# Softmax weights turned by VectorE blocks and HBM instead of TensorE, in a four-layer encoder

## What is computed

```python
# memory attention, in every layer
logits = einsum('bshd,bmhd->bhsm', xq, km)          # 4 heads, 256 x 256
w = softmax(logits, -1)
mem_out = einsum('bhsm,bmhd->bshd', w, vm)
# differential attention, layers 0 and 3
logits = einsum('bqhmd,bkhmd->bmhqk', qb, k) + bias  # 6 heads, two maps each
probs = softmax(logits, -1)
w = probs[:, 0] - lam * probs[:, 1]
o = einsum('bhqk,bkhe->bqhe', w, v)
```

## Time and profile before

| | |
|---|---|
| Time, median of 3 runs | 1245.52 us (1245.37 to 1245.91) |
| Profiled execution: span from first to last instruction | 1244.7 us |
| The profiled execution's own time | not given apart from its span; the median is 0.8 us above the span |
| TensorE busy | 1235.2 us, 99% |
| VectorE busy | 1024.4 us, 82% |
| ACT busy | 730.3 us, 59% |
| DMA, 16 engines | 55.5% of the span, 228 MB |
| Mean granted TensorE clock | 0.998 |

### The profile page before, as it was taken

How to read it: one execution, slowest core, us unless ns; L and a number is a source line. 1 busy time by engine, 2 the same in 40 slices (tenths; PEclk the granted TensorE clock), 3 DMA queues, 4 the chain that set the end, 5 groups by cost and what they waited for, 6 DMA issues and landing times.

```text
span 1244.7 us, 19689 instructions
## 1 busy us (share of the span) xinstructions
PE 1235.2 (99%) x7370; PEld 1082.9 (87%) x7370; DVE 1024.4 (82%) x1599; ACT 730.3 (59%) x1190; POOL 20.1 (2%) x29
## 2 busy tenths in 40 slices
PE   9999999999999999999999999999999999999997
PEld 7988888888999988888889888888888888888886
DVE  5876888889779888988887978988888776988887
ACT  6675765555766546555555546655554774755552
POOL 0001000000000100000000000000000001000000
PEclk9999999999999999999999999999999999999999
DMA  9834576554553345655655764656554533666651
GB/s 333 285 120 136 190 248 190 186 192 163 175 182 119 122 150 169 227 187 195 201 173 168 233 204 162 227 195 199 190 186 169 187 119 119 218 207 201 196 190 54
DMA packets 64539, 229.27 MB, mean 184 GB/s; under 512 B 7575, under 2 KB 9239, under 8 KB 63421
## 3 DMA queue, kind: packets, MB, share of 16 engines
q1 hardware_dynamic: 64444, 228.02, 55.5%
HBM read 226.93 MB, written 1.06 MB: 183 GB/s over the span
## 4 chain that ended last, share of the span: by engine, by line
PE 97%; DMA 1%; SPq 1%; DVE 0%; issue 0%; ACT 0%; DVEq 0%
PE pair L768 28%; PE acc L862 21%; PE pair L771 14%; PE pair L800 4%; PE pair L801 4%; PE pair L802 4%; PE acc L768 2%; PE acc L843 2%; PE acc L842 2%; PE acc L841 2%; PE pair L1022 2%; DMA raw<-in_stream 1%; PE pair L825 1%; PE pair L827 1%; PE pair L829 1%; PE acc L931 1%
## 5 line engine op out<-in xcount | busy, mean ns | idle before, releaser
L1278 DVE TENSOR_TENSOR w_lo<-raw,w_hi 128x1024 fp32r<-128x1024 f32 x400 | 482.6, 1221 | 105.3 <-ACT w_hi L1040 103.7
L1040 ACT ACTIVATE w_hi<-raw 128x1024 fp32r<-128x1024 f32 x400 | 420.5, 1058 | 213.2 <-PE pair L771 70.8
L768 PE MATMUL pair<-xT,w_hi 128*128 128x512 f32 x1520 | 477.8, 396 | 0.0
L771 PEld LDWEIGHTS pair<-xT,w_lo 128*128 128x128 f32 x1520 | 285.5, 188 | 67.2
L771 PE MATMUL pair<-xT,w_lo 128*128 128x256 f32 x1520 | 298.6, 278 | 0.0
L768 PEld LDWEIGHTS pair<-xT,w_hi 128*128 128x128 f32 x1520 | 233.8, 189 | 3.2 <-issue 0.3
L1087 ACT ACTIVATE hid<-pair 128x512 f32<-128x512 f32 x88 | 52.6, 597 | 124.9 <-PE pair L771 124.9
L1319 DVE TENSOR_TENSOR hid<-pair,hid 128x512 f32<-128x512 f32 x88 | 60.7, 690 | 47.9 <-ACT hid L1087 47.7
L800 PE MATMUL pair<-xT,w_hi 128*128 128x256 f32 x336 | 97.8, 291 | 0.0
L801 PE MATMUL pair<-xT,w_hi 128*128 128x256 f32 x336 | 95.0, 283 | 0.0
L802 PE MATMUL pair<-xT,w_lo 128*128 128x256 f32 x336 | 94.9, 283 | 0.0
(11 more groups left out here) (223 smaller groups left out, 1661.9 us busy)
## 6 DMA issues: line engine op xcount, KB each, us to landing
raw<-in_stream SPq DMA_DIRECT2D x400, 512.0 KB, 4.6
gains<-in_ln SPq DMA_DIRECT2D x8, 1024.0 KB, 8.4
bias<-bias_scratch SPq DMA_DIRECT2D x2, 1152.0 KB, 9.0
raw<-in_stream SPq DMA_DIRECT2D x8, 256.0 KB, 6.6
x_tok<-in_x_t SPq DMA_DIRECT2D x4, 256.0 KB, 6.2
y_tok<-in_mem_t SPq DMA_DIRECT2D x2, 512.0 KB, 7.1
x_tok<-in_x SPq DMA_DIRECT2D x1, 1024.0 KB, 6.5
out<-x_tok SPq DMA_DIRECT2D x4, 256.0 KB, 2.0
```

Of the source, the lines that this page charges most:

```text
L768: pe.matmul(bank, w_hi[:, slot, kk * P:(kk + 1) * P], xT[:, kk].rearrange("p a s -> p (a s)"), start=(kk == 0), stop=(kk == KT - 1), skip_ ...
L771: last = pe.matmul(bank[:, 0:SEQ], w_lo[:, slot, kk * P:(kk + 1) * P], xT[:, kk, 0, :], start=False, stop=(kk == KT - 1), skip_group_check ...
L1040: nc.scalar.activation(w_hi[:, u % SPLIT, :], raw[:, u % RAW, :], ACT.Copy).then_inc(hi_ready, 1)
L1278: v.tensor_tensor(w_lo[:, u % SPLIT, :], raw[:, u % RAW, :], w_hi[:, u % SPLIT, :].bitcast(F32), ALU.subtract).then_inc(lo_ready, 1)
```

## The change

The transposes of all eight memory pairs and of heads 0 to 3 of both attention layers leave TensorE; heads 4 and 5 keep theirs. In place of them, VectorE turns each 32x32 block where it lies (`v.transpose`, an item `xswap` or `swap`), and the order of the blocks is put right by a way through HBM. SP stores the tile in four parts of 32 partitions each and fetches it again with the block rows and columns exchanged. For a pair the parts have 32x4x256 values in runs of 1 KB, for a head 32x4x128 in runs of 512 bytes. SP waits for the turned tile, then for the landing of its own stores, and the weight loads of the following units stand behind this in the same list.

The fetched weights of a pair go straight into TensorE's products, which read them in runs of 32 values (a step of a block) with the result put in order by the output's address pattern. Those of a head are put in order by a copy on ACT (`spread`) from `a_sq` into `probT`. Other consequences:

- ACT loses the copies out of PSUM of all pairs and of four heads per attention layer.
- In layer 1 the product of the exponentials with the reciprocal sums goes from VectorE to ACT, as eight scaled copies of 128x256.
- `xpv` comes later: in the attention layers behind halves 9 and 11 instead of 7 and 9, in layer 1 behind 9 and 11 instead of 5 and 7, in layer 2 behind 9 and 11 instead of 5 and 9.
- ACT's exponentials of a later pair of buffers wait until the stores from the same buffer have landed.

The core of the diff:

```diff
+SWAPPED = 4
...
-                  6: [it("exp", 0), it("xturn", 0)], 7: [it("exp", 1), it("xpv", 0)],
-                  8: [it("prob", 0), it("xturn", 1)], 9: [it("prob", 1), it("xpv", 1), it("log", 2), it("log", 3), it("turnw", 0)],
...
+                  8: [it("prob", 0), it("swap", 0)],
+                  9: [it("prob", 1), it("swap", 1), it("fetch", 0), it("fetch", 1), it("xpv", 0), it("log", 2), it("log", 3)],
...
         elif kind == "conv":
...
+                  1: [it("xprob", 0), it("xswap", 0), it("xprob", 1), it("xswap", 1)],
+                  2: [it("xfetch", 0), it("xfetch", 1)], 9: [it("xpv", 0)], 11: [it("xpv", 1)]}
...
-                  4: [it("xturn", 0)], 5: [it("xpv", 0)], 6: [it("xturn", 1)], 7: [it("xpv", 1)]}
+                  2: [it("xswap", 0), it("xswap", 1), it("xfetch", 0), it("xfetch", 1)],
+                  9: [it("xpv", 0)], 11: [it("xpv", 1)]}
...
+            for item in items:
+                name = item[0]
...
+                elif name == "lo":
+                    next_unit(item[1] + RAW)
+                elif name in ("xswap", "swap"):
+                    n = weights_of(item)
+                    sp.wait_ge(swapped, swap_ord[n])
+                    for a in range(4):
+                        rows = slice(32 * a, 32 * a + 32)
+                        sp.dma_start(swap_scratch[n][a].rearrange("b i e -> i b e"), swap_source(n)[rows].rearrange(
+                            "i (b e) -> i b e", b=4)).then_inc(swap_stored[n % 2], 16)
+                elif name in ("xfetch", "fetch"):
...
+                    sp.wait_ge(swap_stored[n % 2], 64 * swap_count[n])
+                    sp.dma_start(swap_target(n), swap_scratch[n].rearrange("a b i e -> (b i) a e")).then_inc(swap_landed[n % 2], 16)
...
-                            last = pe.matmul(bank[64 * i:64 * i + 64, 0:SEQ],
+                            last = pe.matmul(bank[64 * i:64 * i + 64, 0:SEQ].rearrange("p (t a j) -> p t a j", t=2, a=4),
...
-                                             xprobT[:, i, k, :], start=(k == 0), stop=(k == 1))
+                                             weights[:, i, k], start=(k == 0), stop=(k == 1))
...
+                        act.wait_ge(swap_stored[n % 2], 64 * swap_count[n - 2])
...
+                elif name == "xprob" and layer_kind(item[1]) == "hgrn":
+                    n = weights_of(("xswap",) + item[1:])
+                    act.wait_ge(inv_ready, item[2] + 1)
...
+                            last = nc.scalar.activation(prob[:, n % 2, i, t, :], ex[:, n % 2, i, t, :], ACT.Copy,
+                                                        scale=row_inv[:, n % 2, j:j + 1])
...
+                elif name == "spread":
+                    n = prob_ord["", item[1], item[2]]
+                    act.wait_ge(swap_landed[n % 2], 16 * swap_count[n])
...
+                elif name in ("xswap", "swap"):
+                    n = weights_of(item)
+                    of = prob[:, n % 2] if name == "xswap" else prob[:, n % 2, 0:1]
+                    if name == "xswap" and layer_kind(item[1]) == "hgrn":
+                        dve.wait_ge(xprob_ready, item[2] + 1)
+                    v.transpose(swap_source(n).rearrange("p (b c j) -> p c b j", b=4, j=32),
+                                of.rearrange("p i t (k b j) -> p (i t k) b j", k=2, j=32)).then_inc(swapped, 1)
```

More of the change, by code:

```diff
@@ L132, in make_schedule @@
                   19: [it("pv", 4), it("pv", 5), it("ms", 1), it("tok", 1), it("ms", 2)], 20: [it("scale", 1), it("tok", 2)],
                   21: [it("scale", 2)]}
+            if not SWAPPED:
+                at[9] = [it("prob", 1), it("xpv", 0), it("log", 2), it("log", 3), it("turnw", 0)]
+                at[11] = [it("turnw", 1), it("exp", 3), it("prob", 2), it("xpv", 1)]
+                at[13].insert(0, it("turnw", 2))
+                at[15].insert(0, it("turnw", 3))
+                at = {h: [i for i in row if i[0] not in ("swap", "fetch", "spread")] for h, row in at.items()}
@@ L293, in trunk_kernel @@
             banks = ()
-        elif name in ("turn", "xturn"):
+        elif name == "turn":
             banks = (0, 1)
@@ L364, in trunk_kernel @@
             prob = here("prob", [P, 2, 2, 2, SEQ])
-            xprobT = here("xprobT", [P, 2, 2, SEQ])
+            xprobT = here("xprobT", [P, 4 * SEQ])
         with ExitStack() as place:
@@ L502, in trunk_kernel @@
         scratch = nc.dram_tensor("bias_scratch", [HEADS, 512], F32, kind="Internal").ap()
+        swap_scratch = [nc.dram_tensor(f"swap_scratch{n}", [4, 4, 32, 256 if items[pos][0] == "xprob" else 128], F32, kind="Internal").ap()
+                        for n, pos in enumerate(prob_pos)]
         out_dram = out.rearrange("b (t p) d -> p (b t) d", p=P)
@@ L577, in x_count, with swap_source, swap_target @@
             return 2 * (TT * m + t) + h + 1
+        def swap_source(n):
+            s = n % 2
+            return (ex[:, s] if items[prob_pos[n]][0] == "xprob" else prob[:, s, 1:2]).rearrange("p i t s -> p (i t s)")
+        def swap_target(n):
+            name, layer, h = items[prob_pos[n]]
+            if name == "prob":
+                place = a_sq[:, 1 + h % 2]
+            elif h:
+                place = xprobT[:]
+            elif layer_kind(layer) == "attn":
+                place = probT[:, 4:6].rearrange("p h t k s -> p (h t k s)")
+            else:
+                place = prob[:, 0].rearrange("p i t s -> p (i t s)")
+            return place.rearrange("p (a e) -> p a e", a=4)
         def side_bank(pos, k=0):
@@ L619, in load_bias, with next_unit @@
                                               ap=[[1, P], [512, HEADS], [1, 384]])).then_inc(bias_landed, 16)
-            for u in range(RAW, 2 * nchunks):
+            def next_unit(u):
+                if u >= 2 * nchunks:
+                    return
                 c = u // 2
@@ L934, in _ @@
                     last.then_inc(logits_done, 1)
-                elif name == "xturn":
-                    n = prob_ord[pos]
+                elif name == "turnw":
+                    layer, h = item[1:]
+                    n = prob_ord["", layer, h]
                     if ordinal[pos] == 0:
                         pe.wait_ge(ident_landed, 16)
-                    pe.wait_ge(xprob_ready, ordinal[pos] + 1)
-                    for i in range(2):
-                        bank = side(pos, i)
-                        for k in range(2):
-                            for t in range(TT):
-                                last = pe.transpose(bank[:, k * SEQ + t * P:k * SEQ + (t + 1) * P],
-                                                    prob[:, n % 2, i, t, k * P:(k + 1) * P], ident[:])
-                        last.then_inc(xprob_turned, 1)
-                elif name == "turnw":
-                    n = prob_ord[pos]
                     pe.wait_ge(prob_ready, ordinal[pos] + 1)
@@ L1525, in _ @@
                 elif name in ("xprob", "prob"):
-                    n = prob_ord[pos]
+                    n = weights_of((name.replace("prob", "swap"),) + item[1:])
                     s = n % 2
```

126 lines of the change are left out of this document (78 added, 48 removed).

## The result

The changed kernel takes 1250.88 us (median of 4 runs, 1250.42 to 1251.71), against 1245.72 for the kernel before: a ratio of 1.0039, 95% interval 1.0027 to 1.0051. It is 5.2 us slower; 2.7 were forecast. The profiled execution took 1251.2 us, with a span of 1249.4, 4.7 above the span of before. Three executions, two of the kernel before and one of the last experiment, took between 1520 and 3339 us and are left out of every number.

What follows compares the result with a forecast made beforehand. The prediction took TensorE, busy 99% of the span, as the bound. Removing 10.4 us and adding waits of 3.5, 4.1, 4.8 and 0.7 gave +2.7: 1245.5 + 2.7 = 1248.2 us, range 1242 to 1256.

Steps and rivals of the forecast that it cites:

- What is removed: TensorE loses the transposes of eight pairs (0.87 each) and eight heads (0.43 each): 10.4 us.
- Layer 2: Two VectorE transposes delay the gate product that frees a bank for TensorE: wait 3.5 us, against 1.75 won.
- Layer 1: ACT's scalings make the last queries late: TensorE waits 3.8 us at level 0, 0.3 for the gates; 1.75 won.
- The figure without ACT's delay: Layer 1: even without ACT's delay, TensorE would come about 2.2 us ahead of the last queries.
- Layers 0 and 3: Per layer, TensorE waits 1.5 us for ACT's value copy and 0.9 at the head turns; 4.8 in both.
- The queue: Stores and fetches nearly fill the DMA queue in layer 0, making spreads late: 0.7 us in all.
- Transposes: On VectorE, a pair's transpose takes 1.22 us, like a product of that size; a head's half-size one 0.65.
- the rivals with quick and with slow ones: VectorE transposes of about 0.6 us: 1244.6, down to 1243, chance 0.25; of 2.4 us: about 1260, chance 0.05.
- Slow stores: Half-rate stores delay fetches; value products (layers 0, 3) and memory products (0, 2) wait: 1254 to 1257 us, chance 0.2.
- the sum: Whole kernel: −10.4 + 3.5 + 4.1 + 4.8 + 0.7 = +2.7, giving 1248.2 us.
- the likeliest case: Whole kernel: the sum holds, with its own range of 1245.5 to 1251 us; chance 0.38.

Runs made afterwards that it cites:

- the last experiment: Changed kernel with layer 2's second pair turned later, layer 1's products on VectorE with later fetches, and all heads turned by TensorE again: 1243.06 us.
- the filled waits: Changed kernel plus unused TensorE products before the long waits of layers 1 and 2: 1251.62 us with 14 and 13, 1248.72 with 14 and 6.
- the single edits: Changed kernel with one layer edited: layer 2's second pair turned later, 1248.59 us; layer 1's products on VectorE and fetches later, 1247.38 us.
- the combination: Changed kernel with layer 2's second pair turned later, plus layer 1's products on VectorE and its fetches behind halves 4 and 5: 1243.13 us.
- the later fetches: Changed kernel with layer 1's reciprocal-sum products on VectorE and its fetches behind halves 4 and 5 instead of 2: 1247.38 us.
- layer 2's edit: Changed kernel with layer 2's second pair multiplied and turned behind the eighth half, its fetch and the memory products later: 1248.59 us.

## Why the prediction was right, and where its size was off

- **What is removed**, 10.4 forecast. Matched product by product, a pair's transposes gave 0.87 (0.79 at the next product and 0.08 at the one behind it) as forecast, and a head's 0.36 to 0.44, so some 10.1. That reading in runs of 32 values costs nothing, as the prediction put it, is shown too: from the first of eight memory products to the next instruction it is 1.01 us (362.20 to 363.21), as it was before.
- **Layer 2**, 3.5 forecast: wait 3.4. Place, releaser and size as worked; turning one pair later leaves 0.9 and 0.2 of it.
- **Layer 1**, 3.8 and 0.3 forecast: waits of 3.6 and 0.5, at the places named. That ACT's string is the cause is shown: without the scalings 1.2 and 1.4 of the 3.6 are left in the two runs. The figure without ACT's delay, 2.2, was too large.
- **Layers 0 and 3**, 1.5 and 0.9 forecast for each, 4.8 in all. In layer 0 the waits are 1.5 at the value products, behind ACT's value copy, and 0.8 at the head turns, as worked. In layer 3 they are 0.5 and 0.7. (For the 0.8 and the 0.5 the profile names no releaser.) That makes 3.5: what was worked out in layer 0 was carried over to layer 3 without rows of its own, and half of it did not come.
- **The queue**, 0.7 forecast: no wait of TensorE, a spread or a memory product for a fetch. The reason given for a price, a full queue in layer 0, was wrong; where held weight loads cost anything in the experiments it was layers 1 and 2.
- **Transposes** of 1.22 and 0.65 forecast: 1.245 and 0.71. This settles the rivals with quick and with slow ones. The Trainium skill's rule of one element per cycle and lane ("Vector Engine (DVE) Microarchitecture Reference", section 3.8) agrees: a transpose costs like any other pass.
- **Slow stores**: none. In layer 1 eight stores of 128 KB went out within 4.3 us and landed 2.4 us after their issue by the median of all such stores. The Trainium skill's rule that a transfer of 32 partitions reaches half the ports ("SBUF — State Buffer", section "Door 1: The DMA port swizzle") may hold, but at this pace, set by SP's issue, it decided nothing.
- **The step that was mis-sized is the sum.** It priced the waits of layers 1 and 2 by their length alone. In the profiled execution each cost 1.5 us more in products at the lower clock, 3.0 together. With the sizes measured: −10.1 + 3.4 + 1.5 + 3.6 + 0.5 + 1.5 + 3.5 = +3.9, against 4.7 between the spans of the two profiles and 5.2 between the medians; the 0.8 that remain belong to no term. The time lies at the upper end of the range of the likeliest case, 1245.5 to 1251. Matched by layers, 0.5 us were gained before the first changed item, layer 0 is 1.0 and layer 3 2.0 us shorter (1.05 forecast for each, without the queue), layer 1 4.4 and layer 2 3.5 longer (2.35 and 1.75 forecast), and 0.35 were lost ahead of layer 1. That the clock's part is real is shown by the filled waits; it came to 2.2 there in the median.
- **Luck.** The mechanism was right, but the sum is as near as it is partly because errors cancel: 2.0 us too much for layers 0 and 3 and the queue stand against 3.0 for the clock, which no term and no rival had.

Open: the medians of the single edits add up to less than the combination (2.3 and 3.5 against 7.8), while what their profiled executions gained in the layer edited, 3.7 in layer 2 and 4.4 in layer 1, adds up to it. Each single edit leaves one long wait standing, and its price differs: five steps behind the same wait of 3.45 us in layer 2 took 3.57, 5.12 or 5.98 us. That can account for the difference, but it is not shown, since one execution of each kernel was traced. With the later fetches the mean clocks of the runs agree with it (two runs at 0.998 took 1246.1 and 1246.2, three at 0.996 took 1247.5 to 1248.2); with layer 2's edit they do not sort the times. The runs of the single edits scatter over 2.2 to 3.4 us, those of before over 1.7 in the same series.

## What to carry to other kernels

Work that leaves the bounding engine pays only where the engines that take it over have room in that very stage; look at their strings there, not at their share over the span. A wait of a TensorE that is otherwise full can cost more than its length, since the products behind it may run at the lower clock for a while: here up to 2.4 us more behind a wait of 3.45, and nothing in one execution. Waits of at most 1.1 us spread over the layer cost only their length. And when a store, its landing and a fetch share one in-order queue with a stream of loads, issue the fetch late, behind loads that are already due.

## What was unexpected of the hardware

Eleven waits of 2.7 to 4.1 us stand in the traced executions, in a TensorE that is otherwise hardly ever idle. Eight of them were followed, 0.1 to 1.3 us after their end, by some 3.4 us at a granted clock of 0.50; both times in the changed kernel that was worth 1.5 us. In one the lower clock came before the wait's end and stayed twice as long, and two, of 3.45 and of 2.8 us, had no such stretch behind them, though the shortest that had one was 2.7. So the length of a wait alone does not tell whether the clock falls. Single waits of up to 1.6 us never had one, but two of 1.2 and 1.7 us, 5.7 us apart, did.
